# A two-layer backbone with a 64-expert block: units of four kinds of expert room instead of three, and modulation vectors computed elsewhere

## The reference, cut to what matters

```
mod = silu(c) @ w_ada[l] + b_ada[l]                  # six vectors of 1024, once for each of two conditions
sh1, sc1, g1, sh2, sc2, g2 = split(mod, 6)
h   = rmsnorm(x, g[0]) * (1 + sc1) + sh1
fn, q, k, v, hq, hi, hf_fwd, hf_bwd, hg = split(h @ w_in)
mix = concat(fourier(fn), diff_attention(q, k, v), hgrn2(hq, hi, hf_fwd, hf_bwd, hg)) @ w_out
x   = x + g1 * mix
h2  = rmsnorm(x, g[1]) * (1 + sc2) + sh2
eidx = top 8 of the 64 experts of each token, out of the best 4 of 8 groups
routed = sum over the 8 experts of gate_e * (silu(h2 @ w_gate[e]) * (h2 @ w_up[e])) @ w_down[e]
x   = x + g2 * (routed + shared_expert(h2))
```

## Time and profile before

| | us |
|---|---|
| median of 3 runs | 1691.47 (1687.89 to 1701.95) |
| the profiled execution | 1706.42 |
| its span, first to last instruction | 1704.6 |
| PE busy in the span | 1406.1 (82%) |
| DVE / ACT / POOL busy | 671.4 / 408.3 / 256.3 |
| granted TensorE clock, mean over the span | 0.88 of full speed |
| bytes moved by DMA | 378.96 MB, 222 GB/s on the average |

### The profile page before, as it was taken

The page is one execution under the profiler, slowest core; times in us unless marked ns, Lnnn a source line. Parts: engine busy times, 40 slices in busy tenths (PEclk is TensorE's granted clock), DMA queues, the critical chain, the costliest instruction groups (busy, mean ns, idle before and its releaser), DMA issues.

```text
span 1704.6 us, 23713 instructions
## 1 busy us (share of the span) xinstructions
PE 1406.1 (82%) x8772; PEld 962.6 (56%) x8772; DVE 671.4 (39%) x1382; ACT 408.3 (24%) x788; POOL 256.3 (15%) x273
## 2 busy tenths in 40 slices
PE   4799687986999999997059996888889999999942
PEld 2598465954555555554028875676655555555521
DVE  4422767153332222222743347633523222222246
ACT  2324425021222222221013344321112122222201
POOL 1000000001322222231010000000023232322200
PEclk9799857977999999999579996699889999999975
DMA  9553202126988888885874412122469888888853
GB/s 319 206 183 118 105 31 109 50 87 233 362 305 317 328 333 324 305 332 181 340 257 173 141 70 99 41 99 99 180 252 358 333 313 307 324 294 298 328 207 154
DMA packets 126098, 378.96 MB, mean 222 GB/s; under 512 B 28224, under 2 KB 33152, under 8 KB 122784
## 3 DMA queue, kind: packets, MB, share of 16 engines
q1 hardware_dynamic: 86976, 291.31, 46.2%
q0 software_dynamic: 35552, 60.97, 10.1%
q10 hardware_dynamic: 3456, 25.17, 3.6%
HBM read 480.36 MB, written 64.75 MB: 320 GB/s over the span
## 4 chain that ended last, share of the span: by engine, by line
PE 71%; DVE 16%; DMA 6%; issue 4%; ACT 2%; SPq 0%; DVEq 0%; ACTq 0%; POOLq 0%
PE bank L1143 25%; PE bank L1158 11%; PE bank L1129 7%; PE bank L1050 5%; PE bank L771 4%; PE bank L772 4%; PE bank L773 4%; DVE aT L1843 4%; DMA ring<-in_w_ada 3%; DVE aT L1580 1%; PE bank L1066 1%; DMA ring<-in_w_in 1%; PE bank L790 1%; PE bank L1114 1%; PE bank L976 1%
## 5 line engine op out<-in xcount | busy, mean ns | idle before, releaser
L1143 PE MATMUL bank<-slab,xT 128*64 128x256 f32 x2112 | 301.5, 396 | 20.6 <-issue 20.5
L1143 PEld LDWEIGHTS bank<-slab,xT 128*64 128x64 f32 x2112 | 180.6, 142 | 104.2 <-issue 38.2
L732 POOL DMA_INDIRECT sums_scratch<-h,row_table x112 | 112.8, 1007 | 538.6 <-PE bank L1129 438.4
L1826 DVE TENSOR_TENSOR work<-work,bank 128x128 f32<-128x128 f32 x112 | 32.3, 288 | 399.1 <-ACT work L1405 399.1
L1143 PE MATMUL bank<-ring,xT 128*64 128x256 f32 x960 | 152.7, 392 | 9.6 <-issue 9.6
L1158 PE MATMUL bank<-slab,work 128*64 128x512 f32 x528 | 147.3, 592 | 1.5 <-DVE work L1832 1.5
L1405 ACT ACTIVATE work<-bank 128x128 f32<-128x128 f32 x112 | 31.1, 278 | 457.5 <-PE bank L1143 457.5
L1815 DVE COPY h<-bank 128x512 f32<-128x512 f32 x112 | 77.5, 692 | 127.0 <-PE bank L1158 127.0
L1143 PEld LDWEIGHTS bank<-ring,xT 128*64 128x64 f32 x960 | 90.1, 140 | 44.8 <-issue 14.8
L1143 PE MATMUL bank<-h_hi_slot,xT 128*64 128x256 f32 x512 | 108.5, 396 | 6.4 <-issue 6.4
L1492 DVE TENSOR_TENSOR w_lo<-ring,w_hi 128x2048 fp32r<-128x2048 f32 x24 | 55.0, 2292 | 122.3 <-ACT w_hi L1229 122.3
(11 more groups left out here) (334 smaller groups left out, 2324.9 us busy)
## 6 DMA issues: line engine op xcount, KB each, us to landing
slab<-in_w_gate SPq DMA_DIRECT2D x112, 512.0 KB
slab<-in_w_up SPq DMA_DIRECT2D x112, 512.0 KB
slab<-in_w_down SPq DMA_DIRECT2D x112, 512.0 KB
ring<-in_w_ada SPq DMA_DIRECT2D x24, 2048.0 KB
ring<-in_w_gate SPq DMA_DIRECT2D x52, 512.0 KB
ring<-in_w_up SPq DMA_DIRECT2D x52, 512.0 KB
ring<-in_w_down SPq DMA_DIRECT2D x52, 512.0 KB
slab<-sums_scratch ACTq DMA_DIRECT2D x24, 1024.0 KB, 11.5
```

The costliest lines, as they stand in the source:

```text
L732: pool.indirect_dma_start(sums_dram, bass.IndirectOffsetOnAxis(ap=row_table[:, u:u + 1], axis=0), y_rows[:, n % 3, :], None, bounds_check= ...
L1143: last = mm(bk[r, 0:2 * P].rearrange("p (k f) -> p k f", k=2), xT[:, n % 2, j, r], w[:, j, :, :], start=(j == 0), stop=(j == NJ - 1))
```

## The change

What it does, part by part:

1. **Rooms.** 53 units: 8 whole ones (rank 0 to 7, 128 places), 8 *mixed* ones (rank 8 to 15 with 96 places beside rank 56 to 63 with 32), 16 paired ones (64 and 64), 2 *quad* ones (four experts of rank 48 to 55, 32 places each) and 19 spare ones. A room of 96 places is worked in two column tiles, 64 and 32 wide. A whole unit is now one tile of 128 instead of two of 64 with the same weights.
2. **Order of units and loads.** Pair, whole, spare, pair, mixed, spare, eight times; the first time pair, whole, pair, mixed, spare, spare; a quad and a spare after the third and the sixth time, a spare more at the end. 102 loads have a slot and a turn instead of 96.
3. **The place arithmetic.** The first place and the size of the room of each rank are worked out once at the start (rank_col, by_rank), and PE hands them to the experts with a product "rooms", which stands between "ranks" and "owner".
4. **Modulation.** The next layer's first two vectors (m = 6 and 7: its shift and scale) are computed in this layer, around and in attention. m = 2 goes from the projections to the start of the recurrent rounds, m = 3 from there to round 2, m = 4 from behind attention to round 4. The second layer therefore starts with its q and k blocks, which are issued as soon as the ring's slots are free in the expert stage, and splits the q block while the norm is made. The biases and norm gains of both layers are loaded at the start.

The router's counts for the reference's inputs, sorted by size, need no spare window before (every count of rank 16 and above is at most 57 in layer 0 and 60 in layer 1, and the largest of all is 122). With the new rooms one window is needed in layer 0 (rank 48 has 35 tokens, its room 32 places), none in layer 1.

```diff
+def windows_of(unit):
+    if unit < 8:
+        return [(0, P, unit)]
+    if unit < 16:
+        return [(0, 96, unit), (96, P, unit + 48)]
+    if unit < 32:
+        return [(0, WIN, unit), (WIN, P, unit + 16)]
+    if unit < BASE_UNITS:
+        return [(GROUP * k, GROUP * (k + 1), 48 + 2 * k + unit - 32) for k in range(4)]
+    return [(0, WIN, 64 + unit - BASE_UNITS), (WIN, P, 64 + unit - BASE_UNITS + SPARE)]
...
         for turn in range(8):
-            for kind in ("pair", "whole", "pair", "spare", "pair", "whole", "spare"):
+            kinds = ("pair", "whole", "spare", "pair", "mixed", "spare") if turn > 0 else ("pair", "whole", "pair", "mixed", "spare", "spare")
+            for kind in kinds + {2: ("quad", "spare"), 5: ("quad", "spare"), 7: ("spare",)}.get(turn, ()):
                 u = UNITS_BY_KIND[kind].pop(0)
+                tiles = []
+                for lo, hi, w in windows_of(u):
+                    cuts = [lo, 64, hi] if hi - lo == 96 else [lo, hi]
+                    tiles += [(slice(p, q), len(loads)) for p, q in zip(cuts, cuts[1:])]
+                    loads.append((len(order_of_units), w))
...
                     for j in range(NJ):
-                        for half in range(2):
-                            r = slice(WIN * half, WIN * (half + 1))
-                            w = expert_slot(n, half)[0][:, 0:2 * D].rearrange("p (k j f) -> p j k f", k=2, j=NJ)
+                        for r, i in tiles_of_unit[n]:
+                            w = load_slot(i)[0][:, 0:2 * D].rearrange("p (k j f) -> p j k f", k=2, j=NJ)
                             last = mm(bk[r, 0:2 * P].rearrange("p (k f) -> p k f", k=2), xT[:, n % 2, j, r], w[:, j, :, :],
...
-                        for half in range(2):
-                            r = slice(WIN * half, WIN * (half + 1))
-                            last = mm(bk[r, :], actT[:, n % 2, r], expert_slot(n, half)[0][:, 2 * D + c * 512:2 * D + (c + 1) * 512],
+                        for r, i in tiles_of_unit[n]:
+                            last = mm(bk[r, :], actT[:, n % 2, r], load_slot(i)[0][:, 2 * D + c * 512:2 * D + (c + 1) * 512],
...
+            for m in range(2 if l == 0 else 0):
+                blocks += modulation_blocks(l, m)
+            for name, c0 in (("q", Q0), ("k", K0), ("v", V0)):
+                blocks.append((name, [(NJ, 512, 0, in_cols(l, c0, 512))]))
...
+            for m in (2, 3, 4) + ((6, 7) if l + 1 < DEPTH else ()):
+                blocks += modulation_blocks(l, m)
...
-                modulation_product(3)
+                modulation_product(2)
                 for n in range(NLEV):
                     if n == 1:
+                        modulation_turned(2)
+                    if n == 2:
+                        modulation_product(3)
+                    if n == 3:
                         modulation_turned(3)
+                    if n == 4:
+                        modulation_product(4)
...
+                if l + 1 < DEPTH:
+                    modulation_product(6)
...
+                    if l + 1 < DEPTH and u == 3:
+                        modulation_turned(6)
+                    if l + 1 < DEPTH and u == 5:
+                        modulation_product(7)
+                    if l + 1 < DEPTH and u == 8:
+                        modulation_turned(7)
...
-                modulation_product(4)
...
+                bk = banks.claim(pe, "rooms")
+                banks.wait_emptied(pe, "ranks")
+                for k in range(3):
+                    last = mm(bk[:, k * E:(k + 1) * E], by_rank[:, k * P:(k + 1) * P], of_rank[0:E, :], start=True, stop=True)
+                banks.filled(last, "rooms")
...
                 squares_of_x(x_ready.at(l, 0))
-                rows_of_modulation(0)
+                if l == 0:
+                    rows_of_modulation(l, 0)
+                else:
+                    split(range(0, 2))
                 root_of_mean("ms1")
```

More of the change, by code:

```diff
@@ L31 @@
 BASE = 8
-LAYER_DVE = 159
 NSLOT = 2
@@ L48, with steps_by_rank @@
               ("c_lat", 512), ("s_lat", 512), ("tie", 64))
+def windows_of(unit):
[8 more added lines that the diff above has]
+    return [(0, WIN, 64 + unit - BASE_UNITS), (WIN, P, 64 + unit - BASE_UNITS + SPARE)]
+def steps_by_rank(value, slope):
+    out = []
+    for r in range(1, len(value)):
+        if value[r] != value[r - 1] + slope:
+            out.append((r, value[r] - value[r - 1] - slope))
+    return out
+BY_RANK = sorted((r, unit * P + lo, hi - lo) for unit in range(BASE_UNITS) for lo, hi, r in windows_of(unit))
+PLACE_STEPS = steps_by_rank([place for _, place, _ in BY_RANK], P)
+ROOM_STEPS = steps_by_rank([room for _, _, room in BY_RANK], 0)
 def const_offsets():
@@ new lines, in trunk_program @@
+        landed, fix_sum = [[] for _ in range(DEPTH)], [[0] * NSLOT for _ in range(DEPTH)]
+        for l in range(DEPTH):
+            for b, (_, parts) in enumerate(fixed[l]):
+                fix_sum[l][b % NSLOT] += 16 * len(parts)
+                landed[l].append(fix_sum[l][b % NSLOT])
+        UNITS_BY_KIND = {"whole": list(range(8)), "mixed": list(range(8, 16)), "pair": list(range(16, 32)),
+                         "quad": list(range(32, BASE_UNITS)), "spare": list(range(BASE_UNITS, NUNITS))}
@@ L534, in trunk_program, with slot_before @@
                 order_of_units.append(u)
[L535 removed]
+        assert all(w < E for _, w in loads[:XSLOT])
+        assert sorted(order_of_units) == list(range(NUNITS)) and sorted(w for _, w in loads) == list(range(E + NXW))
         def slot_uses(s):
             return sum(1 for i in range(len(loads)) if i % XSLOT == s)
[L540 removed]
+        def slot_before(l, r):
+            return sum(fix_sum[k][r] + 48 * slot_uses(XSLOT - NSLOT + r) for k in range(l))
@@ new lines, in trunk_program, with reads_to @@
+        last_fill = [{block_of(l, "out", 1): ("out", NJ - 1)} for l in range(DEPTH)]
+        for l in range(DEPTH):
+            for m in range(8):
+                if ("ada%d" % m) in [n for n, _ in fixed[l]]:
+                    last_fill[l][block_of(l, f"ada{m}", 1)] = (f"ada{m}", 1)
+        def reads_to(l, b):
+            return sum(1 for k in range(b) if k not in last_fill[l] and k not in split_blocks[l])
+        reads_before = [sum(reads_to(k, len(fixed[k])) for k in range(l)) for l in range(DEPTH)]
@@ L1457, in _, with modulation @@
             nc.vector.memset(tick[:, :], 0.0).then_inc(x_ready.sem, 1)
-            order.leave()
-            def modulation(m):
+            def modulation(l, m):
                 for half in range(2):
@@ L1501, in _ @@
             for l in range(DEPTH):
-                order.enter("layer", l)
                 banks.enter("layer", l)
```

437 lines of the change are left out of this document (214 added, 223 removed).

## The result

The changed kernel takes 1915.62 us (median of 4 runs, 1905.68 to 1920.74), against 1693.8 us for the kernel before in its 4 runs: ratio 1.130, 95% interval 1.123 to 1.137. It is 13% slower. The profiled execution took 1915.23 us, 0.4 us from the median of its runs; that of before lay 12.6 us above the median of the 4.

The account below looks back on a forecast made before the run. PE bounds the kernel, with the DMA engines also close to full in the expert stages. Profiled 1706.4 + 191 (expert stages) − 8 (elsewhere) = 1889 us, lowered for the 15 us above median to 1870; range 1825 to 1905, wider 1760 to 1915.

Parts of the forecast that it names:

- The likeliest case: Whole kernel: width changes and load waits in the expert stages outweigh the saved units; 1870 us, chance 0.72.
- B: Expert stages: no drain between tiles 64 and 32 wide, loads bind; 1777 us, chance 0.13.
- C: Expert stages: drain, but loads arrive at 412 GB/s without gap and waits stay near 55 + 6; 1771 us, chance 0.05.
- The mixed unit: PE in the expert stages: each width change empties the array; 7.7 us more a unit, +124 for 16.
- rival D: Expert stages: mixed units overlap and new waits equal the old; 1644 us, chance 0.06.
- Rival E: Expert stages: as forecast, and mixed units half empty by drains run at the lower clock; 1960 us or above, chance 0.04.
- Whole and quad units at no cost: PE in the expert stages: one matmul of 128 columns or four of 32 priced at nothing extra.
- The waits: Expert stages: waits for weights at mixed units, quads and pairs behind quads, with slow starts; +106 us, bounds 0 and +130.
- Three units fewer, −39: PE in the expert stages: three fewer units of 6.45 us in each of two layers; −39 us.
- Expert stages, +191: Both expert stages in all: fewer units −39, mixed units +124, waits with slow starts +106; +191 us.
- Outside the stage, −8: Place arithmetic +3 and moved modulation, with an earlier second-layer start; −8 us in sum, bounds −30 and +10.
- From the profiled execution to the median, −15: Whole kernel: the profiled execution ran 15 us above the median of the runs, so 1889 became 1870.

Follow-up runs that it names:

- the run with one width: The changed kernel with rooms of 96 places worked in three tiles of 32 columns instead of 64 and 32; 1823.37 us, ratio 1.068.

## Why the prediction was right, and where its sizes were off

Forecast 1870 us, measured 1915.6. The likeliest case with its mechanism was the right one. The time was not hit as well: it is 10.6 us above the range of that case (1825 to 1905) and lies at the very end of the wider one (1760 to 1915), which had been drawn to take in the faster rivals B and C. By the prediction's own steps:

- *The mixed unit.* Right in kind and size: 9.05 us for `up` exactly, 3.82 for `down` where 3.97 was worked out, +7.5 a unit instead of +7.7. The choice of the high end, that 64 beside 32 behaves as 64 beside 128, was the one that mattered, and rivals B and D fall with it. Rival E falls too: the clock was 0.94 and 0.93 over the stages, and a mixed unit without a wait in front took 9.05 at a granted clock of 1.00. (The changes of width in the trace of before are 258 by count, not 280; none starts earlier than 0.07 before an end.)
- *Whole and quad units at no cost.* Right; `up` of a whole unit takes 3.45 and the `down` behind it 1.87, together what 3.60 and 1.72 were, and four tiles of 32 take 3.59 where no wait is in front (the run with one width).
- *The waits.* Right in place. In front of the mixed units of layer 0 they are 5.3, 2.8, 4.7, 3.4, 3.1, 3.0 and 1.3, mean 3.4 for a forecast of 3.9; in front of the quads 10.0 for 9.4; behind them 9.3 and 8.3 for 7.6. With all kinds the sum is 130.0 for 122. Rival C falls.
- *Three units fewer, −39.* Right as a term of this sum, in which the longer waits stand as a term of their own: PE is busy 107 us longer in the two stages, for −39 + 124 + 20 of slow starts = 105. As a gain that the rooms would bring without the mixed units' cost (rival D) it is not shown: in the orders that were tried 53 units took as long as 56.
- *Expert stages, +191.* Measured +200; 9 too low, of which 8 are the waits. `up` of a mixed unit behind a wait takes 9.1 to 11.9 us, 1.4 more than 9.05 in the mean of the seven of layer 0, for the 1.3 I took.
- *Outside the stage, −8.* Measured +9 in the profiles (+18.6 in front of the first stage, −9.7 between the stages), 17 off: this is the term that was mis-sized most. The second layer's start was right and better (from the end of the stage to the first projection 74.2 us instead of 96.4, −22 for −19, with 5 of them from an earlier read of the sums). From the last output of the recurrence to the output projection layer 0 takes 60.6 us instead of 46.6, 14 more instead of 11: the two products and turns stand there, and the hole behind attention that had hidden a product is left empty. And 6.5 us came from a step that the prediction did not have, the wait for a bank in front of the shared expert; the plan of the banks changed with the order, and I read that as bookkeeping. The shared expert with the first product of the places then took 16.3 and 18.0 us instead of 13.9 in each layer, another 6.5 that the prediction did not have. The rest is made of smaller terms both ways; the earlier q block brought 3.3 us in layer 0 instead of 6 (first projection at 59.0 instead of 62.3).
- *From the profiled execution to the median, −15.* The forecast for a profiled execution, 1889, is 26 from 1915, and these 26 are the 9 and the 17 above. The −15 turns the sum into one on before's median of 1691, which is a fair step, but the changed kernel's profiled execution lay at its own median, so that the 15 stayed in the error; 1889 − 15 was then rounded from 1874 down to 1870. The runs of before spread over 14 us and those of after over 15, and the range of 1825 to 1905 had no room for it beside the errors of the terms.

## What to carry to other kernels

Before giving matmuls of small output tiles to one pass, look whether all neighbours have one width: equal tiles start 0.01 us apart, and at each change of width the next matmul waited here until 0.07 us before the end of the last, so that a room of 96 is better worked as three tiles of 32 (3.59 us) than as 64 and 32 (9.05 us). Where two resources are close to full in one stage, work taken from one of them can come back as waits for the other, as it did here; the order in which loads with few slots follow each other can cost more (61 and 66 us in the two layers here) than the work saved. When work moves out of a place, look what it had been filling there, and which buffers the plan now gives to whom.

## What the runs showed of the hardware that was not expected

Tiles of 64 and 32 columns do not overlap although they lie in disjoint columns of the array and write disjoint parts of a bank: at all 312 changes between them the next started 0.06 to 0.07 us before the last one's end, and in two groups they took 7.17 us for what equal tiles do in 3.6. The transfers of the expert stage, weights and gathers together, kept at 354 GB/s with the DMA engines at 0.96 of their time over 50 us, and yet fell behind a demand that a reckoning from rows of five loads had called covered. And an earlier start of the expert stage is sometimes kept and sometimes lost: one that began 6.1 us sooner ended at the same time, others that began 16.2 and 16.6 us sooner ended 13.6 and 15.4 sooner. What decides this the runs don't show.
